# Three x tiles ahead of their low parts behind a layer norm, and one sigmoid for the hybrid attention's gates

## The reference, cut to what matters

```python
def hybrid_layer(x, mem, ...):
    x = layer_norm(ALPHA * x + 0.5 * swiglu_ffn(x, ffn1_w_in, ffn1_w_out), ln1_g, ln1_b)
    h = x @ w_in
    g_ssd, g_att, z, xbc, dt_raw, q, c_kv, q_idx, k_idx, w_idx = split_cols(h, IN_SPLITS_2)
    y_ssd = ssd_branch(z, xbc, dt_raw, ...)
    y_att = dsa_branch(q, c_kv, q_idx, k_idx, w_idx, ...)     # top-64 keys of 256, then 16 heads of softmax attention
    merged = sigmoid(g_ssd) * (y_ssd @ w_proj_ssd) + sigmoid(g_att) * (y_att @ w_proj_att)
    x = layer_norm(ALPHA * x + merged @ w_out, ln2_g, ln2_b)
    x = layer_norm(ALPHA * x + memory_xattn(x, mem, w_mq, w_mkv, w_mo), ln3_g, ln3_b)
    x = layer_norm(ALPHA * x + 0.5 * swiglu_ffn(x, ffn2_w_in, ffn2_w_out), ln4_g, ln4_b)
```

## Time and profile before

| | |
|---|---|
| median of 3 runs | 3482.73 us (3475.93 to 3483.59) |
| the profiled execution, its time | 3478.66 us |
| its span, first to last instruction | 3476.8 us |
| instructions | 63489 |
| share of the span PE / DVE / ACT / POOL is busy | 93% / 52% / 44% / 26% |
| granted TensorE clock, mean | 0.937 |
| stages that the change touches, us from the span's start | first `Ffn` 1306 to 1501, `Hybrid` 1510 to 1913, `Mem` 1913 to 2045, second `Ffn` 2054 to 2249 |
| `pick` / the 16 waves | 1765 to 1781 / 1781 to 1861 |

### The profile page before, as it was taken

How to read it: one execution, slowest core, us unless ns; L and a number is a source line. 1 busy time by engine, 2 the same in 40 slices (tenths; PEclk the granted TensorE clock), 3 DMA queues, 4 the chain that set the end, 5 groups by cost and what they waited for, 6 DMA issues and landing times.

```text
span 3476.8 us, 63489 instructions
## 1 busy us (share of the span) xinstructions
PE 3245.4 (93%) x27080; PEld 3105.9 (89%) x27080; DVE 1795.9 (52%) x3066; ACT 1517.5 (44%) x2518; POOL 910.2 (26%) x486
## 2 busy tenths in 40 slices
PE   9998999998797999988978889999999999999998
PEld 8996999996687999988967889999889999996998
DVE  5446555548664545356565444454445446445543
ACT  5444444544223544447454444354334444443442
POOL 3321232331342332312211123222213322222222
PEclk9988999998898999999987999999899999997899
DMA  6542354554202555533432435445323544440353
GB/s 234 185 155 71 133 183 165 187 178 141 64 3 75 187 172 181 188 133 106 150 103 79 140 126 184 165 149 174 116 79 122 176 164 146 164 158 25 122 175 116
DMA packets 133385, 484.50 MB, mean 139 GB/s; under 512 B 14959, under 2 KB 17151, under 8 KB 132399
## 3 DMA queue, kind: packets, MB, share of 16 engines
q1 hardware_dynamic: 131120, 470.25, 40.3%
q0 software_dynamic: 1984, 10.19, 0.9%
HBM read 479.34 MB, written 1.05 MB: 138 GB/s over the span
## 4 chain that ended last, share of the span: by engine, by line
PE 83%; DVE 8%; ACT 4%; issue 3%; POOL 1%; DMA 0%; DVEq 0%; POOLq 0%; ACTq 0%
PE ps L179 82%; ACT hi L176 1%; ACT arena L176 1%; DVE lo L159 1%; PE ps L187 1%; DVE tmp L167 1%; ACT L176 1%; DVE arena L159 1%; DVE yT L167 1%; POOL small L159 1%; DVE arena L167 1%; DVE small L173 1%; DVE tmp L164 0%; ACT xT L176 0%; POOL arena L159 0%
## 5 line engine op out<-in xcount | busy, mean ns | idle before, releaser
L179 PE MATMUL ps<-hh,lo 128*128 128x256 f32 (+1 forms) x4624 | 1336.9, 289 | 0.0
L179 PE MATMUL ps<-hh,hi 128*128 128x256 f32 (+1 forms) x4336 | 1266.5, 292 | 62.7 <-DVE hl L167 27.0
L179 PE MATMUL ps<-hl,hi 128*128 128x256 f32 (+1 forms) x4336 | 1255.1, 289 | 0.0
L159 POOL TENSOR_TENSOR lo<-raw,hi 128x1024 fp32r<-128x1024 f32 x271 | 690.2, 2547 | 1843.0 <-ACT hi L176 1842.9
L176 ACT ACTIVATE hi<-raw 128x1024 fp32r<-128x1024 f32 x814 | 852.0, 1051 | 448.9 <-PE ps L179 339.3
L159 DVE TENSOR_TENSOR lo<-raw,hi 128x1024 fp32r<-128x1024 f32 x543 | 697.3, 1287 | 562.4 <-ACT hi L176 541.7
L179 PEld LDWEIGHTS ps<-hh,hi 128*128 128x128 f32 x4336 | 844.8, 195 | 75.7 <-DVE hl L167 28.9
L179 PEld LDWEIGHTS ps<-hh,lo 128*128 128x128 f32 x4624 | 898.6, 194 | 0.0
L179 PEld LDWEIGHTS ps<-hl,hi 128*128 128x128 f32 x4336 | 842.6, 194 | 0.2
L179 PE MATMUL ps<-hfh,lo 128*128 128x256 f32 (+1 forms) x1760 | 499.0, 284 | 0.0
L179 PE MATMUL ps<-hfh,hi 128*128 128x256 f32 (+1 forms) x1520 | 430.8, 283 | 0.0
(11 more groups left out here) (361 smaller groups left out, 3792.9 us busy)
## 6 DMA issues: line engine op xcount, KB each, us to landing
raw<-in_l_ffn_w_gate SPq DMA_DIRECT2D x88, 512.0 KB, 3.6
raw<-in_l_ffn_w_up SPq DMA_DIRECT2D x88, 512.0 KB, 4.1
raw<-in_l_ffn_w_down SPq DMA_DIRECT2D x88, 512.0 KB, 3.7
raw<-in_g SPq DMA_DIRECT2D x88, 512.0 KB, 3.2
raw<-in_u SPq DMA_DIRECT2D x88, 512.0 KB, 3.3
raw<-in_d SPq DMA_DIRECT2D x88, 512.0 KB, 3.3
raw<-in_ffn_w_gate SPq DMA_DIRECT2D x44, 512.0 KB, 4.2
raw<-in_ffn_w_up SPq DMA_DIRECT2D x44, 512.0 KB, 4.3
```

The source lines that it names most:

```text
L159: return self.e.tensor_tensor(o, a, b, op)
L179: return self.e.matmul(o, a, b, start=first, stop=final, skip_group_check=loose)
```

## The change

(1) `Split` updates three tiles of x (`AHEAD`) before the first low part, where it updated one; with the update that stands ahead of each low part in the loop, four updates instead of two stand ahead of low part 0. (2) The gates leave PSUM with a plain copy, in place; one sigmoid over all eight tiles stands behind the waves on ACT, and DVE's multiplications wait for it (`gs`) instead of for each gate (`ga`). (3) `W.lo(dve, self.u3 + 5)` moves from behind `pick` to its fifth round; in the waves the low parts of the weights stand behind the low part of the output instead of ahead of it.

```diff
@@ class Split
+    AHEAD = 3
     def dve(self, dve):
         K, T = self.K, self.T
-        self.prev.upd_dve(dve, 0)
+        for k in range(self.AHEAD):
+            self.prev.upd_dve(dve, k)
         for k in range(8):
-            if k < 7:
-                self.prev.upd_dve(dve, k + 1)
+            if k + self.AHEAD < 8:
+                self.prev.upd_dve(dve, k + self.AHEAD)
             dve.wait_ge(*self.prev.x(k))
@@ class Hybrid, act
             if i in self.LATE:
                 self.gate(act, self.EARLY + self.LATE.index(i))
+
+        act.wait_ge(*self.ga(7))
+        act.act(self.gatt, self.gatt, ACT.Sigmoid).then_inc(self.gs.h, 1)
         self.datt.act(act)
@@ gate
-        act.act(self.gatt[:, self.GATT[x], :], self.gbank(x)[:, 0:T1], ACT.Sigmoid).then_inc(self.ga.h, 1)
+        act.act(self.gatt[:, self.GATT[x], :], self.gbank(x)[:, 0:T1], ACT.Copy).then_inc(self.ga.h, 1)
@@ class Hybrid, dve
         self.pick(dve)
-        W.lo(dve, self.u3 + 5)
         for i in range(22):
             if 1 < i < 18:
                 self.probs(dve, i - 2)
             if i < 16:
                 self.rowmax(dve, i)
-            if i in self.LATE:
-                W.lo(dve, self.u3 + self.EARLY + self.LATE.index(i) + 6)
             if i > 5:
                 ...
+            if i in self.LATE:
+                W.lo(dve, self.u3 + self.EARLY + self.LATE.index(i) + 6)
@@ behind the waves
-                dve.wait_ge(*self.ga(self.GATT.index(k)))
+                dve.wait_ge(*self.gs(0))
@@ pick
         for r in range(8):
+            if r == 4:
+
+                K.W.lo(dve, self.u3 + 5)
             dve.turn()
```

More of the change, by code:

```diff
@@ L2278, in __init__ @@
             K.sig(x, n) for x in ("scores", "rowmax", "exps", "probs", "turned", "pta", "pv", "oh", "ol")]
-        self.ga = sg("hy_gatt", 8)
+        self.ga, self.gs = sg("hy_gatt", 8), sg("hy_gsig", 1)
         self.datt = Down(K, T1, "w_proj_att_2", self.oT, 8, lambda k: self.ol(8 + k))
```

## The result

The changed kernel takes 3459.8 us (median of 4, 3457.24 to 3462.57), the kernel before beside it 3481.2 (median of 4). The ratio is 0.9945, 95% interval 0.9933 to 0.9957: -19.1 us (-23.3 to -15.0); the two medians are 21.4 apart. The profiled execution took 3458.20 us.

A forecast was written before the change was run, and what follows sets the result against it. PE, busy 3245.4 of 3476.8 us, bounds the kernel, so only its waits and clock count. +1.7 - 0.1 - 6.4 - 7.4 = -12.2 us, from 3482.73 to 3470.5; range 3463 to 3480.

The forecast's parts named there:

- Gate projection 3 inside `pick`: Waves' start: with its low part in round 5 the projection runs at once at the high level, 1775.8 to 1778.6.
- the sigmoid hidden: ACT behind the waves: load 1.3 us and sigmoid 2.0 to 3.0 fit into 5.87 us of idle; cost 0.
- RMS entry: First feed-forward: low part 0 behind four updates delays PE, nothing later absorbs it; +1.7 us, bounds +1.2 to +2.2.
- `Mem`: Entry of `Mem`: third projection's copy comes in time, idle and slow clock go; -6.4 us, bounds 4.5 to 6.9.
- A: `Mem` gives little, since the seventh or eighth projection finds another wait, POOL's low part; -5.8 in all, 3476.9; chance 0.06.
- D: Layer norm's entry: three tiles ahead do not speed it, ACT bounds at 1.77 per tile; -5.7, 3477.0; chance 0.04.
- B: Waves bound by PE and DVE, shorter ACT work only makes PE idle and slow; -6.8, 3475.9; chance 0.08.
- C: ACT behind the waves: sigmoid delays `datt`'s high parts; 3490 or more; chance 0.04 with whatever else is slower.
- Waves: Low parts moved and fewer table loads give a lead that stays to the end: -7.4 us, bounds -4.0 to -9.7.
- Gate projection 4: Waves: starts at 1782.9 instead of 1787.7, at the low level after 3.2 us idle, 2.3 longer; 2.5 lead at its end.
- `datt`'s start: Behind the waves: forecast change 0.
- theory 5: Recorded for a follow-up: the delay behind the RMS norm removes the low stretch near 1668; -4 to -5 us against before.

The follow-up runs named there:

- part 1 alone: Three tiles of x ahead of their low parts at all four entries, rest as the kernel before: ratio 0.9975, -8.7 us (-11.5 to -5.6).
- RMS only: Three tiles ahead only at the entry behind the RMS norm, against the kernel before: ratio 0.9998, -0.7 us (-3.8 to +2.4).
- parts 2 and 3: Gate copies with one sigmoid and the moved low parts, `Split` as in the kernel before: ratio 0.9973, -9.4 us (-13.2 to -5.9).
- unread matmuls: Changed kernel plus PE matmuls nobody reads, 24 in turn 9 and 8 in turns 10 to 15: 0.9935 of before, median 3455.35 us.
- `Hybrid`'s entry alone: Three tiles ahead at the entry of `Hybrid` only, against the kernel before: ratio 0.9997, -1.0 us (-4.9 to +2.8).

## Why the prediction was wrong, step by step

**The mechanisms were right.** Gate projection 3 inside `pick`, the load ahead of exp(0), 44 loads, the sigmoid hidden, low part 0 of the RMS entry 1.70 later, 6.3 us in `Mem` up to its eighth projection. Rivals A and D did not come: no wait took the old one's place in `Mem`, and the layer norm's entry went at 0.71 us a tile. B did not come either: shorter ACT work pulled PE along. C stayed away by 0.35 us of ACT's time.

**The step that failed is the clock.** The forecast treated it as a property of a place: where nothing was changed, the low stretches of the trace before stay, and where it had to choose, it took the low level. By the table the surplus over -12.2 is 8.5 us in the profiled execution (measured 6.9, interval 2.8 to 11.1):

- Waves, -11.1 for -7.4, a term that was mis-sized and lies below its own bound of -9.7. Gate projection 4 was taken at the low level, 2.3 us longer, because PE would idle 3.2 us ahead of it. PE idled 2.09, for the scores of wave 1 ran ahead of that wait and not behind it, and the projection ran at the high level. So it started 5.9 us earlier for the forecast's 4.8 and ended 5.9 earlier for 2.5. Part of that is lost in the wait behind it: at projection 5 the lead is 6.1 for 4.4. The other 2.0 come in the turns behind, with less low time: projection 5 leaves the low level sooner (0.8), and from 1803 (trace before) to `datt` PE has 34 us of low time for 43.
- `datt`'s start, -2.3 for 0: its first matmuls ran at the low level before, 0.21 us apart, and at the high one after. All kernels with an edit in the waves' low parts have the -2.3; the one with nothing changed behind 1310 us has 0.8.
- The middle of `Hybrid`, -3.1 for 0, and 0.6 at its entry. This comes with the delay behind the RMS norm and with nothing else that I changed: the seven profiled executions with two or three tiles ahead there lack the stretch, and the ten with one, that of before among them, have it.
- The RMS entry, +0.9 for +1.7: PE's wait was right (its first matmul comes 1.70 later), but "nothing later absorbs it" was not. The low stretch there begins in the idle time and ends at the same distance from its start in both kernels, so the later start spends less of its work in it: 0.8 came back within 7 us.
- `Mem`, -4.1 for -6.4: two low stretches of 1.6 each behind the term, 1.0 less at the next entry. In the trace before they are absent; kernels that reach `Mem` earlier for another reason have them too, and lose 2.2 to 3.5 there. Against such a kernel the same term is -6.4 (part 1 alone less RMS only) or -7.6 (changed less parts 2 and 3).

**What comes with the delay near 1668.** The low stretches at 1504, 1549 and 1583 begin in all 17 profiled executions at the same distances from the start of the one at 1306 (198.0, 242.3 and 276.5 us); the work does not. The one near 1668 begins, in the ten that have it, 361.8 us behind that start. PE isn't idle there: it is 2.2 to 2.3 us into a run of 32 matmuls of one column. In the seven kernels with the delay the work stands some 0.3 us later, so at the same instant PE is only 1.75 to 1.95 us into that run, and the clock stays high. The run, kernel before and changed (timelines of PE):

```profile
1665.82 4.80 PE L179 MATMUL ps<-cst,sq 128*128 128x1 f32 x32
```
```profile
1663.64 3.63 PE L179 MATMUL ps<-cst,sq 128*128 128x1 f32 x32
```

This fits theory 5, and no trace here has a case between the two groups.

**What stays open.** Whether the shift of 0.3 us is the cause, which only a kernel that moves this run and nothing else could show. And how large it is in the mean: -4.2 in the trace of the RMS entry alone, -0.7 (-3.8 to +2.4) in its times. Executions of one kernel differ by up to 17 us (96 of before, in all comparisons behind the first: 3467.2 to 3484.7), which a trace of one execution does not show. That the sign of the RMS term is minus in the changed kernel rests on medians 4.4 and 4.5 us apart and on the traces, not on the ratio.

**The rules cited.** No run shows the drain of 1.38 us that the Trainium skill (ScalarE: Activation LUTs, What ACT_TABLE_LOAD costs) adds to a load: in the changed kernel the load starts 0.02 us behind the high part's end, and exp(0) again 1.29 us after it. The Trainium skill (TensorE: Matmul & The Clock Gate, What's actually happening) has activity hold the clock; the trace agrees, in the unread matmuls: 0.56 without, 1.00 with them. The forecast leant on the same passage for a slow projection 4, and there 2.09 us of idle left the clock high.

## What to carry to other kernels

Where the clock changes level many times, a trace of one execution prices each idle time, but not which low stretches come along; put a term for them into the range on both sides (here 8.5 us of 20.7), and look for one wherever PE stops for a microsecond or two or runs matmuls of one column, behind the change too. Cut the stall at the head of a pipeline first: one moved instruction of DVE gave 5 of 19 us, seven table loads alone 1.7, not clear of zero. Where PE must wait in a loop that it bounds itself, work that nobody reads can pay: 5 us here in the trace, 3.5 by the ratios.

## What the runs showed of the hardware

Low stretches mostly come again from execution to execution, of different kernels too, as long as the code ahead of them is timed alike: the kernel with `Hybrid`'s entry alone has all stretches of the table within 0.2 us of before, though its first 1200 us took 2.1 us longer. They do not always: the changed kernel's two executions differ by 0.5 us in the waves. Where no instruction differs they come and go mostly in steps of 0.8, 1.6, 2.3 and 3.1 us, not by degrees. PE idle for 2.09 us kept the high level (1776.10); the loop with 0.93 us of idle in 3.82 ran at the low one (changed kernel, turn at 1816.06); and near 1668 the clock fell with PE busy throughout, 20.00 of 20.00 us, on matmuls of one column. And a load of Sigmoid's table with 2048 columns per partition after it took 3.2 us, 1.92 of it the sigmoid, a little under the lower of the two bounds taken from rows.
